# Three seven-product pairs instead of two in each of three FFNs, with some sums made by accumulating transfers

## The chip, the cores and the metric

The kernel runs as one program on one core of a Trainium2 chip. The core has a matrix engine (PE; its weight loads are the row PEld), a vector engine (DVE), a scalar engine (ACT), GpSimd (POOL) and a sync engine (SP), and 16 DMA engines that move data between HBM and the on-chip memory. SP and ACT hand transfers to hardware queues, POOL hands them to a software queue. The metric is device time in microseconds (us) of one execution, as a median over runs.

## The reference

A 256-token, 1024-wide activation goes through three blocks. Each has a mixer and then a gated feed-forward network (FFN); the three FFNs are where the change is made. All arithmetic is float32.

```python
def swiglu(u, w_in, w_out):
    gt, up = jnp.split(u @ w_in, 2, axis=-1)
    return (jax.nn.silu(gt) * up) @ w_out

# layers 0 and 1:  h = h + mixer(rmsnorm(h));  h = h + swiglu(rmsnorm(h, norm_ffn), ffn_w_in, ffn_w_out)
# third block:     x = x + (silu(h2 @ ffn_w1) * (h2 @ ffn_w3)) @ ffn_w2
```

The hidden width is 2816, so an FFN multiplies 256x1024 by 1024x5632 and then 256x2816 by 2816x1024.

## The kernel before, in words

**Units.** Weights come in units of 128 partitions x 1024 floats (512 KB), each as two transfers of 256 KB issued by SP (L466) into a ring of six slots, `raw`. To keep float32 accuracy every unit is split into a high and a low half: ACT writes `whi`, the rounded copy (L631), and DVE then writes `wlo = raw - whi` over `raw` (L1175; the two names share one memory). PE multiplies three times: high by high, activation-low by weight-high, and high by weight-low. So an ordinary unit is 12 matmuls, 8 that need `whi` alone and then 4 that need `wlo` too. Every engine works through the units in one order and counts them in semaphores (`hi_ready`, `lo_ready`, `unit_used`); SP loads unit u once PE has used unit u-6.

**An FFN.** It has 11 blocks of 256 hidden columns. Block j has four "up" units (gate and up columns side by side) and, one block later, two "down" units. `PLAN` writes out the order of all units; ACT, DVE, PE and SP each have a hand-written sequence that follows it (`body`, `pair`, `feed`).

**A pair.** At j in `PAIRED` two neighbouring blocks are done together by a Strassen-type scheme: seven products of half-size operands instead of eight. The four parts of the two blocks' weights (b11, b12, b21, b22, 1 MB each) are loaded into `work` (L510) and DVE makes four sums t1 to t4 from them (L1294, eight instructions of 128x1024 for one pair; t3 takes the place of b12). Each of the seven products is two units of six matmuls (PE lines L2309, L2311, L2314); ACT and DVE split them as they split raw units (L648, L1189). After the 14 half-product units, in whose midst two down units stand, come four up units of block j+2 and four down units. In what follows, b0 to b23 are these 24 units of a pair: b0 to b5, b8 to b15 the half products, b16 to b19 the up units, b20 to b23 the down units. The parts of the second pair are loaded during the first one (`PART_LOADS`).

**Hidden columns.** After each block ACT applies silu, DVE multiplies, PE transposes (`hid_turn`, L2259), ACT copies (L689) and DVE subtracts (L1259); the next down unit waits for that.

**POOL** issues a few loads of tables at the start of the program (L562 to L601) and does nothing in the FFNs.

Of the kernel before, what the change touches and what calls it, by code (L numbers as in the profile page):

```python
# [58 lines left out]
PAIRED = (4, 8)  # L59
# [30 lines left out]

PARTS = [f"{b}_{i}" for b in ("b11", "b12", "b22", "b21") for i in range(2)]
_p0 = plan_at("pair", 0, "b11", 0)
PART_LOADS = {}
for _i, _name in enumerate(PARTS):
    PART_LOADS.setdefault(6 + 2 * _i, []).append((0, _name))
for _i, _name in enumerate(PARTS[:4]):
    PART_LOADS.setdefault(_p0 + 7, []).append((1, _name))
for _i, _name in enumerate(PARTS[4:]):
    PART_LOADS.setdefault(_p0 + 18 + _i, []).append((1, _name))
# [3 lines left out]
for _k in range(len(PAIRED)):  # L103
    SUMS += [f"{_k}_{_t}_{_i}" for _t in ("t1", "t3", "t2", "t4") for _i in range(2)] + [f"{_k}_{_c}" for _c in ("c22", "c11", "c21")]
# [16 lines left out]
              for i, unit in enumerate(PLAN) if unit[0] == "pair"}  # L121

# [128 lines left out]
def build(nc, D, out):  # L251
    with ExitStack() as ctx:
# [28 lines left out]
        rhalf = sb("rhalf", [P, 6, NT])  # L281
        rq_a = sb("rq_a", [P, 64])
# [116 lines left out]

        F_a = W(0, 2048).rearrange("p (k t) -> p k t", k=KT)  # L400
# [18 lines left out]

        def tap(name, n):  # L420
# [8 lines left out]
        half_used = sem("half_used")  # L429
        evac_act, evac_dve = sem("evac_act"), sem("evac_dve")  # L430
# [22 lines left out]
        def _(sp):  # L453
# [33 lines left out]
            def load_ffn(u0, gate_w, gate_n0, up_w, up_n0, down_w):  # L487
# [8 lines left out]
                for i, unit in enumerate(PLAN):  # L496
# [6 lines left out]
                    for pair, name in PART_LOADS.get(i, ()):  # L503
                        b, h = name.split("_")
                        if pair:

                            sp.wait_ge(lo_ready, u0 + plan_at("pair", 0, "t3" if b == "b12" else b, int(h)) + 1)
# [53 lines left out]
        def _(pool):  # L561
# [13 lines left out]
            for half in range(2):  # L575
# [3 lines left out]
            nc.gpsimd.dma_start(A_dec, D["decay"]).then_inc(sem("decay_loaded"), 16)  # L579
            nc.gpsimd.dma_start(posi[:, :], D["positions"][0].rearrange("(t p) -> p t", p=P), allow_slow_non_contiguous=True)\  # L580
                .then_inc(sem("pos_loaded"), 16)
# [16 lines left out]
            for i in range(4):  # L598
# [3 lines left out]
                if i >= 2:  # L602
                    filter_fold(i - 2)


        @block.scalar
        def _(act):
# [25 lines left out]
            def feed(n):  # L633

                for u in range(fed[0], n):
                    if u in PAIR_UNITS:
                        pair_hi(u, *PAIR_UNITS[u])
                    else:
                        split_hi(u % RING, loaded(u), unit_width(u))
                fed[0] = max(fed[0], n)  # L640

            def pair_hi(u, n, k, name, half):
                act.wait_ge(unit_used, u - RING + 1)
                if name[0] == "b":
                    act.wait_ge(part_loaded[name], parts_there(n, k, name))
                else:
                    act.wait_ge(sem("pair_sums"), sums_done(n, f"{k}_{name}_{half}"))
# [32 lines left out]
            def ffn(n, u0, norm):  # L680
# [18 lines left out]
                def silu_of(t, src):  # L699
                    a_(sil[:, t, :], src, ACT.Silu, scale=rstd[:, norm, t:t + 1]).then_inc(sil_ready, 1)  # L700
# [16 lines left out]
                def pair(k, j):  # L717
# [12 lines left out]
                    silu_of(1, F_part[:, 2, 0:256])  # L730
                    feed(b + 17)
                    act.wait_ge(unit_used, b + 14)
                    silu_of(0, ps[0][:, 0:256])
# [4 lines left out]
                    turn(j + 1 + FB * n, 2)  # L738
# [3 lines left out]
                    turn(j + 2 + FB * n)  # L742
                    feed(b + 22)
# [14 lines left out]
                last = u0 + FFN_UNITS - 2  # L758
                feed(last + 2)
                turn(FB * (n + 1), 2)  # L760
                feed(min(last + 5, U_END))
# [399 lines left out]
        def _(dve):  # L1161
# [55 lines left out]
            def row_scale(n):  # L1217
# [3 lines left out]
                rsqrt(rstd[:, n, :], NT)  # L1221
                v_.tensor_scalar(rhalf[:, n, :], rstd[:, n, :], 0.5, None, ALU.mult).then_inc(rstd_ready, 1)
# [27 lines left out]
            def ffn(n, u0, norm, use):  # L1250
# [14 lines left out]
                def token_sum(name):  # L1265
# [6 lines left out]
                    else:  # L1272
                        a11, a12, a21, a22 = (F_a[:, r, c] for c in (slice(0, P), slice(P, S)) for r in (slice(0, 4), slice(4, 8)))
                        x0, x1, op, need = {"s1": (a21, a22, ALU.add, "a1"), "s2": (F_s[:, 0, :, :], a11, ALU.subtract, "s1"),
                                            "s3": (a11, a21, ALU.subtract, "a1"),
                                            "s4": (a12, F_s[:, 1, :, :], ALU.subtract, "s2")}[name]
                        dve.wait_ge(sem("pair_sums"), sums_done(n, need))
                        ins = v_.tensor_tensor(F_s[:, i - 1, :, :], x0, x1, op)
# [7 lines left out]
                def weight_sum(k, name, i):  # L1286

                    x0, x1 = {"t1": ("b12", "b11"), "t3": ("b22", "b12"), "t2": ("b22", "t1"), "t4": ("b21", "t2")}[name]
                    for b in (x0, x1):
                        if b[0] == "b":  # L1290
                            dve.wait_ge(part_loaded[b], parts_there(n, k, b))
                    if x1[0] == "t":
                        dve.wait_ge(sem("pair_sums"), sums_done(n, f"{k}_{x1}_{i}"))
                    v_.tensor_tensor(pair_part(f"{name}_{i}"), pair_part(f"{x0}_{i}"), pair_part(f"{x1}_{i}"), ALU.subtract)\  # L1294
                        .then_inc(sem("pair_sums"), 1)

                def body(j):
                    b = u0 + plan_at("up", j, 0)
                    k = 0 if j < PAIRED[0] else 1
                    away = (PAIRED[k] - j) if j < PAIRED[k] else 0  # L1300
# [11 lines left out]
                    elif away == 2:  # L1312
                        weight_sum(k, "t1", 0)
                        feed(b + 4)
                        weight_sum(k, "t1", 1)
                        feed(b + 5)
                        turn(j + FB * n)
                        feed(b + 6)
                        weight_sum(k, "t3", 0)
                        feed(b + 7)  # L1320
                        hidden(2 * j + 2 * FB * n)
                        weight_sum(k, "t3", 1)
                        return
                    elif away == 1:
                        weight_sum(k, "t2", 0)
                        feed(b + 4)
                        weight_sum(k, "t2", 1)
                        feed(b + 5)
                        turn(j + FB * n)
                        feed(b + 6)  # L1330
                        weight_sum(k, "t4", 0)
                        feed(b + 7)
                        weight_sum(k, "t4", 1)
# [6 lines left out]
                def hid_of(t, src, count):  # L1340
                    dve.wait_ge(sil_ready, count)
                    v_.scalar_tensor_tensor(hid[:, t, :], src, rstd[:, norm, t:t + 1], sil[:, t, :],
# [5 lines left out]
                def pair(k, j):  # L1348
# [13 lines left out]
                    hid_of(1, F_part[:, 2, 256:512], hids + 1)  # L1362
                    feed(b + 16)
                    hid_of(0, ps[0][:, 256:512], hids + 2)
                    feed(b + 17)
                    dve.wait_ge(unit_used, b + 16)
# [8 lines left out]
                    if more:  # L1375
                        weight_sum(k + 1, "t1", 0)
                    feed(b + 20)
                    if more:
                        weight_sum(k + 1, "t1", 1)
                    turn(j + 2 + FB * n)  # L1380
                    feed(b + 21)
                    if more:
                        weight_sum(k + 1, "t3", 0)
# [3 lines left out]
                    if more:  # L1387
                        weight_sum(k + 1, "t3", 1)
# [10 lines left out]
                last = u0 + FFN_UNITS - 2  # L1399
                feed(last + 2)  # L1400
                turn(FB * (n + 1), 2)
                feed(min(last + 5, U_END))
# [17 lines left out]
            v_.memset(sign[0:64, :], 1.0).then_inc(sem("sign_set"), 1)  # L1420
# [1551 lines left out]
```

## Time and profile before

| | |
|---|---|
| median of 3 runs | 1043.28 us (1042.96 to 1043.73) |
| span of the profiled execution | 1041.3 us |
| PE busy | 1033.9 us, 99% of the span, 4884 matmuls and transposes |
| DVE busy | 843.5 us, 81% |
| ACT busy | 593.8 us, 57% |
| POOL busy | 21.6 us, 2% |
| PE clock granted | nine tenths or more in every one of the 40 slices |
| bytes moved | 182.97 MB, 176 GB/s over the span |

The profile is one execution; its page gives the span from the first to the last instruction, 2.0 us under the median of the three runs. PE is busy almost throughout, so time is lost or won where PE does fewer instructions or where it has to wait. Matmuls overlap in the rows: each is shown some 390 ns long while the next begins some 227 ns later, so distances between starts are what counts.

### The profile page before, as it was taken

The numbers are of one execution on the slowest core, as the hardware profiler recorded it, in microseconds if no ns is written. First come the engines' busy times: TensorE is split into PE (matmuls) and PEld (weight loads), VectorE is DVE, ScalarE is ACT, GpSimd is POOL, SyncE is SP. The second block draws the span as 40 slices with busy tenths as digits, with TensorE's granted clock in tenths as the row PEclk, the third lists the DMA queues.
The fourth block names the chain that finished last, engine by engine and source line by source line (L and its number), as shares of the span: only waits on it lengthen the run. The fifth ranks groups of instructions, "written<-read, shape, count | busy, mean of one in ns | idle before, by whom it ended". The sixth has DMA issues, their size and how long they took to land.

```text
span 1041.3 us, 13328 instructions
## 1 busy us (share of the span) xinstructions
PE 1033.9 (99%) x4884; PEld 841.5 (81%) x4884; DVE 843.5 (81%) x1366; ACT 593.8 (57%) x897; POOL 21.6 (2%) x30
## 2 busy tenths in 40 slices
PE   9999999999999999999999999999999999999998
PEld 7877778888888888788888888787777888888887
DVE  6877889797868987896887788989978878878684
ACT  6845474655646646655656564638656446466462
POOL 0221000000000000000000000000000000000000
PEclk9999999999999999999999999999999999999999
DMA  8762478382456534683743653544444468739243
GB/s 278 228 206 83 128 249 270 122 277 87 142 187 187 180 134 142 216 283 126 246 140 96 221 169 122 158 151 154 147 160 135 148 189 258 242 122 303 85 153 107
DMA packets 135706, 182.97 MB, mean 176 GB/s; under 512 B 12588, under 2 KB 82730, under 8 KB 135514
## 3 DMA queue, kind: packets, MB, share of 16 engines
q1 hardware_dynamic: 134130, 178.36, 53.2%
q0 software_dynamic: 1104, 3.21, 1.2%
q8 instruction: 39, 0.64, 0.3%
q10 hardware_dynamic: 408, 0.56, 0.2%
q14 instruction: 25, 0.20, 0.1%
HBM read 181.03 MB, written 1.05 MB: 175 GB/s over the span
## 4 chain that ended last, share of the span: by engine, by line
PE 92%; DVE 5%; ACT 2%; issue 1%; DVEq 0%; ACTq 0%
PE ps L2169 13%; PE ps L2174 13%; PE ps L2170 13%; PE ps L2186 7%; PE ps L2187 7%; PE ps L2191 7%; PE ps L2309 4%; PE ps L2311 4%; PE ps L2314 4%; PE ps L2152 3%; PE ps L2154 3%; PE ps L2153 3%; DVE wlo L1175 1%; PE ps L2259 1%; PE ps L2242 1%; PE ps L2733 1%
## 5 line engine op out<-in xcount | busy, mean ns | idle before, releaser
L1175 DVE TENSOR_TENSOR wlo<-raw,whi 128x1024 fp32r<-128x1024 f32 (+1 forms) x290 | 349.4, 1232 | 28.8 <-ACT whi L631 27.1
L631 ACT ACTIVATE whi<-raw 128x1024 fp32r<-128x1024 f32 (+1 forms) x290 | 295.5, 1053 | 106.9 <-DMA raw<-in_ffn_w_in 33.1
L2169 PE MATMUL ps<-whi,ath 128*128 128x512 f32 (+1 forms) x688 | 274.5, 400 | 2.2 <-ACT whi L631 0.7
L2170 PE MATMUL ps<-whi,atl 128*128 128x512 f32 (+1 forms) x688 | 266.4, 388 | 0.0
L2174 PE MATMUL ps<-wlo,ath 128*128 128x512 f32 (+1 forms) x688 | 182.9, 388 | 0.0
L2169 PEld LDWEIGHTS ps<-whi,ath 128*128 128x128 f32 x688 | 129.3, 188 | 35.6 <-issue 5.9
L2174 PEld LDWEIGHTS ps<-wlo,ath 128*128 128x128 f32 x688 | 128.2, 188 | 27.4 <-DVE wlo L1175 0.6
L2170 PEld LDWEIGHTS ps<-whi,atl 128*128 128x128 f32 x688 | 129.4, 188 | 24.7 <-issue 0.5
L2186 PE MATMUL ps<-whi,brh 128*128 128x512 f32 x272 | 106.5, 392 | 0.0
L2187 PE MATMUL ps<-whi,brl 128*128 128x512 f32 x272 | 105.9, 389 | 0.0
L1189 DVE TENSOR_TENSOR wlo<-work,whi 128x1024 fp32r<-128x1024 f32 x84 | 98.7, 1220 | 4.5 <-ACT whi L648 4.5
L648 ACT ACTIVATE whi<-work 128x1024 fp32r<-128x1024 f32 x84 | 83.8, 1053 | 7.8 <-PE ps L2191 7.8
L2191 PE MATMUL ps<-wlo,brh 128*128 128x512 f32 x272 | 72.7, 389 | 0.0
L1259 DVE TENSOR_TENSOR brl<-ps,brh 128x512 fp32r<-128x512 f32 x33 | 22.7, 689 | 53.3 <-ACT brh L689 53.1
L2186 PEld LDWEIGHTS ps<-whi,brh 128*128 128x128 f32 x272 | 51.1, 188 | 11.1 <-issue 0.3
L2191 PEld LDWEIGHTS ps<-wlo,brh 128*128 128x128 f32 x272 | 51.1, 188 | 10.7
L2187 PEld LDWEIGHTS ps<-whi,brl 128*128 128x128 f32 x272 | 51.1, 188 | 10.3
L1294 DVE TENSOR_TENSOR work<-work 128x1024 f32<-128x1024 f32 x48 | 58.5, 1219 | 0.5 <-DMA work<-in_ffn_w_in 0.4
L689 ACT ACTIVATE brh<-ps 128x512 fp32r<-128x512 f32 x33 | 19.6, 594 | 59.1 <-PE ps L2259 59.1
L655 ACT ACTIVATE ath<-ps,gcol 128x256 fp32r<-128x256 f32 x56 | 22.7, 473 | 37.6 <-PE ps L2242 37.6
L1197 DVE SCALAR_TENSOR_TENSOR atl<-ps,gcol,ath 128x256 fp32r<-128x256 f32 x56 | 23.9, 479 | 21.2 <-ACT ath L655 21.2
L2309 PE MATMUL ps<-whi,sum_hi 128*128 128x512 f32 x96 | 38.0, 396 | 0.0
(380 smaller groups left out, 1415.4 us busy)
## 6 DMA issues: line engine op xcount, KB each, us to landing
raw<-in_ffn_w_in SPq DMA_DIRECT2D x112, 256.0 KB, 3.5
raw<-in_w_in SPq DMA_DIRECT2D x104, 256.0 KB, 2.9
raw<-in_ffn_w SPq DMA_DIRECT2D x100, 256.0 KB, 3.5
raw<-in_ffn_w_out SPq DMA_DIRECT2D x88, 256.0 KB, 3.5
work<-in_ffn_w_in SPq DMA_DIRECT2D x64, 256.0 KB, 4.8
raw<-in_a_w_in SPq DMA_DIRECT2D x48, 256.0 KB, 4.3
raw<-in_b_w_in SPq DMA_DIRECT2D x48, 256.0 KB, 3.1
work<-in_ffn_w SPq DMA_DIRECT2D x32, 256.0 KB, 4.6
```

Of the source, the lines that this page charges most:

```text
L631: a_(unit_view(whi, slot, w), unit_view(raw, slot, w), ACT.Copy).then_inc(hi_ready, 1)
L648: a_(unit_view(whi, u % RING, 512), pair_part(f"{name}_{half}"), ACT.Copy).then_inc(hi_ready, 1)
L1175: v_.tensor_tensor(unit_view(wlo, slot, w), unit_view(raw, slot, w), unit_view(whi, slot, w), ALU.subtract).then_inc(lo_ready, 1)
L1189: v_.tensor_tensor(unit_view(wlo, u % RING, 512), pair_part(f"{name}_{half}"), unit_view(whi, u % RING, 512), ALU.subtract).then_inc(lo_re ...
L1294: v_.tensor_tensor(pair_part(f"{name}_{i}"), pair_part(f"{x0}_{i}"), pair_part(f"{x1}_{i}"), ALU.subtract)\
L2169: mm(ps[bk + apart * t][:, 0:w], ath[:, k, t * P:(t + 1) * P], rh[:, kk, :], start=k == 0, stop=False)
L2170: mm(ps[bk + apart * t][:, 0:w], atl[:, k, t * P:(t + 1) * P], rh[:, kk, :], start=False, stop=False)
L2174: ins = mm(ps[bk + apart * t][:, 0:w], ath[:, k, t * P:(t + 1) * P], rl[:, kk, :], start=False, stop=k == KT - 1)
L2186: mm(o, act_h[:, k, t * P:(t + 1) * P], rh[:, nb, :], start=first, stop=False)
L2187: mm(o, act_l[:, k, t * P:(t + 1) * P], rh[:, nb, :], start=False, stop=False)
L2191: ins = mm(ps[banks[2 * nb + t]][:, :], act_h[:, k, t * P:(t + 1) * P], rl[:, nb, :], start=False, stop=last)
L2309: mm(ps[bank][:, :], hi[:, 2 * i + kk, :], rh[:, kk, :], start=not onto and i + kk == 0, stop=False, skip_group_check=onto)
```

## The change

It changes the three FFNs, and four things in them.

1. `PAIRED` goes from (4, 8) to (3, 6, 9): three pairs in each FFN. After a pair the next one follows at once, and the last pair has no up units behind it, so its two blocks' down units come straight after its products.
2. The signs of the sums are turned so that t1, t2 and t4 are plain additions of whole parts: three DVE instructions of 128x2048 for one pair instead of eight of 128x1024. Two of the products come out negated, and `rneg`, the negated row scale, puts that right.
3. t3 = b12 + b22 is made by POOL: one accumulating transfer of 1 MB from on-chip memory to on-chip memory.
4. For the two down units b20 and b21 after the first and the second pair of each FFN (`ADDED`, 12 units in all) DVE's subtraction is left out. ACT writes `wlo = -whi` over `raw`, and POOL then adds the weights again from HBM onto it, by two accumulating transfers of 256 KB for each unit. PE waits for these transfers in `low_there`.

The parts of the next pair are also asked for at other places of SP's order, and some semaphores of the mixers are merged.

```diff
-PAIRED = (4, 8)
+PAIRED = (3, 6, 9)
+
+ACC_ROW = 2048
...
-            plan += [("up", j + 2, c) for c in range(4)]
-            plan += [("down", j + b, k) for b in range(2) for k in range(2)]
+            if j + 2 < FB:
+                plan += [("up", j + 2, c) for c in range(4)]
+                plan += [("down", j + b, k) for b in range(2) for k in range(2)]
+            else:
+                plan += [("down", j, k) for k in range(2)]
...
+for _k in range(len(PAIRED)):
+    _at = (6, 7, 8, 9, 10, 11, 13, 15)
+    if _k:
+        _at = [plan_at("pair", _k - 1, "b11", 0) + n for n in (8, 9, 10, 11, 17, 18, 19, 20)]
+    for _i, _name in zip(_at, PARTS):
+        PART_LOADS.setdefault(_i, []).append((_k, _name))
...
+ADDED = [u0 + plan_at("pair", k, "b11", 0) + i for u0 in (U_F0, U_F1, U_F2) for k, j in enumerate(PAIRED) if j + 2 < FB
+         for i in (20, 21)]
...
+            def add_low(n, k):
...
+                for m, u in enumerate(ADDED):
+                    if first <= u < first + 24:
+                        pool.wait_ge(neg_ready, m + 1)
+                        if m >= 2:
+                            pool.wait_ge(lo_added[m % 2], 32 * (m // 2))
+                        _, j, k2 = PLAN[u - (U_F0, U_F1, U_F2)[n]]
+                        v, row = unit_view(wlo, u % RING, 512), (2 * j + k2) * P
+                        for nb in range(2):
+                            nc.gpsimd.dma_start(v[:, nb, :], down_w[row:row + P, nb * 512:(nb + 1) * 512],
+                                                accum_op=ALU.add).then_inc(lo_added[m % 2], 16)
+
+            for n in range(3):
+                for k in range(len(PAIRED)):
+                    pool.wait_ge(sem("pair_sums"), sums_done(n, f"{k}_t1"))
+                    pool.wait_ge(part_loaded["b22"], parts_there(n, k, "b22"))
+                    nc.gpsimd.dma_start(pair_whole("t3"), pair_whole("b22"), accum_op=ALU.add, max_dma_last_dim=ACC_ROW)\
+                        .then_inc(sem("pair_t3_added"), 16)
+                    add_low(n, k)
...
+                    if u in ADDED:
+                        a_(unit_view(wlo, u % RING, 512), unit_view(raw, u % RING, 512), ACT.Copy, scale=-1.0)\
+                            .then_inc(neg_ready, 1)
...
+                elif name == "t3":
+                    act.wait_ge(sem("pair_t3_added"), t3_there(n, k))
...
-                    else:
+                    elif u not in ADDED:
                         split_lo(u % RING, u + 1, unit_width(u))
...
+            def low_there(n):
+
+                if n - 1 in ADDED:
+                    m = ADDED.index(n - 1)
+                    pe.wait_ge(lo_added[m % 2], 32 * (m // 2 + 1))
+                else:
+                    pe.wait_ge(lo_ready, low(n))
...
+                    if j + 2 == FB:
+                        product(b + 14, 1, *a22, onto=True, middle=lambda: hid_turn(hids + 2))
+                        pe.wait_ge(hid_lo, j + 1 + FB * n)
+                        down_unit((b + 16) % RING, 2, False, False, b + 17, brh, brl)
+                        hid_turn(hids + 4)
+                        down_unit((b + 17) % RING, 3, False, False, b + 18, brh, brl)
+                        return
```

How the order moves is seen at three places. The first is SP's queue around the end of the first pair of the first FFN, before: `raw<-` are a unit's two transfers, `work<-` the two of half a part of the next pair.

```order
L466 DMA raw<-in_ffn_w_in 128x2x256 x6
L510 DMA work<-in_ffn_w_in 128x2x256 x2
L466 DMA raw<-in_ffn_w_in 128x2x256 x2
L510 DMA work<-in_ffn_w_in 128x2x256 x2
L466 DMA raw<-in_ffn_w_out 128x512 x2
L510 DMA work<-in_ffn_w_in 128x2x256 x2
L466 DMA raw<-in_ffn_w_out 128x512 x2
```

And the same place now.

```order
L488 DMA raw<-in_ffn_w_in 128x2x256 x4
L534 DMA work<-in_ffn_w_in 128x2x256 x2
L488 DMA raw<-in_ffn_w_in 128x2x256 x2
L534 DMA work<-in_ffn_w_in 128x2x256 x2
L488 DMA raw<-in_ffn_w_in 128x2x256 x2
L534 DMA work<-in_ffn_w_in 128x2x256 x2
L488 DMA raw<-in_ffn_w_out 128x512 x2
L534 DMA work<-in_ffn_w_in 128x2x256 x2
L488 DMA raw<-in_ffn_w_out 128x512 x10
```

Before b20, the first `in_ffn_w_out` unit, SP asked for six others of 512 KB from b16 on (four up units, two halves of parts); now for seven (four and three). Before b21 it was eight, and is nine.

The second place is ACT at the same point, before, from the last two up units of the pair on (`brh` is the turned hidden block, `sil` the silu).

```order
L631 ACTIVATE whi<-raw 128x1024 x2
L689 ACTIVATE brh<-ps 128x512
L631 ACTIVATE whi<-raw 128x1024 x2
L700 ACTIVATE sil<-ps,rstd 128x256 x2
L631 ACTIVATE whi<-raw 128x1024 x7
```

And now.

```order
L679 ACTIVATE whi<-raw 128x1024 x2
L742 ACTIVATE brh<-ps 128x512
L679 ACTIVATE whi<-raw 128x1024
L689 ACTIVATE wlo<-raw 128x1024
L679 ACTIVATE whi<-raw 128x1024
L689 ACTIVATE wlo<-raw 128x1024
L753 ACTIVATE sil<-ps,rstd 128x256 x2
L679 ACTIVATE whi<-raw 128x1024 x2
L701 ACTIVATE whi<-work 128x1024 x6
```

Behind each high half of b20 and b21 stands its negated copy, and the next pair's parts (`whi<-work`) follow after b22 and b23.

The third place is POOL's queue in the FFNs, of which nothing stood there before; these are the rows of the first FFN and the first row of the next.

```order
+L649 DMA work<-work 128x4x512
+L642 DMA wlo<-in_ffn_w_out 128x512 x4
+L649 DMA work<-work 128x4x512
+L642 DMA wlo<-in_ffn_w_out 128x512 x4
+L649 DMA work<-work 128x4x512 x2
```

The t3 of the second and of the third pair (`work<-work`) are issued behind the four additions of the pair ahead of each; POOL takes them in this order alone.

## Rows read from the trace of the kernel before

**Rows 1.** The page: busy time, clock, and the chain that ended last.

```profile
PE 1033.9 (99%) x4884; PEld 841.5 (81%) x4884; DVE 843.5 (81%) x1366; ACT 593.8 (57%) x897; POOL 21.6 (2%) x30
...
PEclk9999999999999999999999999999999999999999
...
PE 92%; DVE 5%; ACT 2%; issue 1%; DVEq 0%; ACTq 0%
```

**Rows 2.** Timeline of PE, low products of b20 and b21 (start, length).

```profile
232.27 1.07 PE L2191 MATMUL ps<-wlo,brh 128*128 128x512 f32 x4
...
234.99 0.39 PE L2191 MATMUL ps<-wlo,brh 128*128 128x512 f32 x1
```

**Rows 3.** Timeline of ACT: high halves of b20 and b21 in the first pair.

```profile
225.17 0.60 ACT L689 ACTIVATE brh<-ps 128x512 fp32r<-128x512 f32 x1 [0.94 <-PE ps L2259]
226.01 1.06 ACT L631 ACTIVATE whi<-raw 128x1024 fp32r<-128x1024 f32 x1 [0.24 <-DMA raw<-in_ffn_w_out]
228.87 1.06 ACT L631 ACTIVATE whi<-raw 128x1024 fp32r<-128x1024 f32 x1 [1.79 <-DMA raw<-in_ffn_w_out]
```

**Rows 4.** Timeline of SP's queue: b16 to b18 asked for, later b20.

```profile
212.01 3.60 SPq L466 DMA_DIRECT2D raw<-in_ffn_w_in  x6
...
218.73 1.45 SPq L466 DMA_DIRECT2D raw<-in_ffn_w_out  x2
```

**Rows 5.** Windows: busy time in each, PE clock, share of the DMA engines, GB/s.

```profile
193.30:241.30 48.00, 48.00 (x219) 39.73 (x218) 39.17 (x42) 29.05 (x35) 0.00 (x0) 1.00 0.76 250
220.00:232.00 12.00, 12.00 (x56) 9.94 (x55) 11.64 (x14) 6.73 (x10) 0.00 (x0) 1.00 1.07 370
26.00:40.00 14.00, 14.00 (x92) 11.94 (x91) 10.73 (x22) 9.09 (x13) 7.80 (x15) 1.00 1.01 280
52.00:60.00 8.00, 8.00 (x35) 5.77 (x34) 6.53 (x8) 3.53 (x5) 1.07 (x2) 1.00 0.78 226
```

**Rows 6.** Timeline of ACT: two high halves in a row.

```profile
211.15 2.00 ACT L648 ACTIVATE whi<-work 128x1024 fp32r<-128x1024 f32 x2
```

**Rows 7.** POOL's transfers: size, median us from issue to landing.

```profile
con<-in_consts POOLq DMA_DIRECT2D x4, 290.0 KB, 3.2
...
work<-in_decay POOLq DMA_DIRECT2D x1, 512.0 KB, 7.9
```

**Rows 8.** Line L576, POOL's two loads of 512 KB: issue (ns, starts), landing.

```profile
L576 POOL DMA_DIRECT2D work<-in_filt_w x2: 523/524/526, 25.6 to 26.1; - x2
...
DMA to landing us min/median/max: 5.2/6.2/7.2
```

**Rows 9.** Timelines of POOL and DVE while POOL issues a transfer.

```profile
53.20 0.54 POOL L601 DMA_DIRECT2D con<-in_consts  x1 [17.86 <-DVE work L1485]
...
52.82 2.35 DVE L1175 TENSOR_TENSOR wlo<-raw,whi 128x1024 fp32r<-128x1024 f32 x2
```

**Rows 10.** Groups of DVE's instructions in the whole run (count, busy, mean ns).

```profile
L1175 DVE TENSOR_TENSOR wlo<-raw,whi 128x1024 fp32r<-128x1024 f32 (+1 forms) x290 | 349.4, 1232 | 28.8 <-ACT whi L631 27.1
L1189 DVE TENSOR_TENSOR wlo<-work,whi 128x1024 fp32r<-128x1024 f32 x84 | 98.7, 1220 | 4.5 <-ACT whi L648 4.5
L1294 DVE TENSOR_TENSOR work<-work 128x1024 f32<-128x1024 f32 x48 | 58.5, 1219 | 0.5 <-DMA work<-in_ffn_w_in 0.4
```

**Rows 11.** Timelines of PE and DVE at the end of the second pair's products.

```profile
281.75 0.39 PE L2309 MATMUL ps<-whi,ath 128*128 128x512 f32 x1
...
281.39 0.48 DVE L1342 SCALAR_TENSOR_TENSOR hid<-ps,rstd,sil 128x256 f32<-128x256 f32 x1 [1.31 <-ACT sil L700]
```

**Rows 12.** Timeline of PE and DVE: first matmul after b23; a sum for the next pair.

```profile
241.34 0.39 PE L2169 MATMUL ps<-whi,ath 128*128 128x512 f32 x1
...
223.29 1.22 DVE L1294 TENSOR_TENSOR work<-work 128x1024 f32<-128x1024 f32 x1
```

More of the change, by code:

```diff
@@ L91 @@
 PARTS = [f"{b}_{i}" for b in ("b11", "b12", "b22", "b21") for i in range(2)]
-_p0 = plan_at("pair", 0, "b11", 0)
 PART_LOADS = {}
[L94 to L99, printed above, removed]
+for _k in range(len(PAIRED)):
[4 more added lines that the diff above has]
+        PART_LOADS.setdefault(_i, []).append((_k, _name))
 SUMS = ["a0", "a1", "s1", "s2", "s3", "s4", "l1", "l2", "l3", "l4"]
 for _k in range(len(PAIRED)):
-    SUMS += [f"{_k}_{_t}_{_i}" for _t in ("t1", "t3", "t2", "t4") for _i in range(2)] + [f"{_k}_{_c}" for _c in ("c22", "c11", "c21")]
+    SUMS += [f"{_k}_{_t}" for _t in ("t1", "t2", "t4")] + [f"{_k}_{_c}" for _c in ("c22", "c11", "c21")]
 COPIES = 4 + 3 * len(PAIRED)
@@ L121, with low @@
               for i, unit in enumerate(PLAN) if unit[0] == "pair"}
+ADDED = [u0 + plan_at("pair", k, "b11", 0) + i for u0 in (U_F0, U_F1, U_F2) for k, j in enumerate(PAIRED) if j + 2 < FB
+         for i in (20, 21)]
+assert all(PLAN[(u - U_F0) % (U_F1 - U_F0)][0] == "down" for u in ADDED if u < U_B)
+def low(n):
+    return n - sum(u < n for u in ADDED)
 C_COLS = ((768, 512), (1280, 512), (0, 512), (512, 256), (1792, 512), (2304, 512), (2816, 512), (3328, 512))
@@ L281, in build @@
         rhalf = sb("rhalf", [P, 6, NT])
+        rneg = sb("rneg", [P, 6, NT])
         rq_a = sb("rq_a", [P, 64])
@@ L429, in build @@
         half_used = sem("half_used")
+        neg_ready, lo_added = sem("neg_ready"), [sem(f"lo_added{i}") for i in range(2)]
         evac_act, evac_dve = sem("evac_act"), sem("evac_dve")
@@ L505, in load_ffn @@
                         if pair:
-                            sp.wait_ge(lo_ready, u0 + plan_at("pair", 0, "t3" if b == "b12" else b, int(h)) + 1)
+                            sp.wait_ge(lo_ready, low(u0 + plan_at("pair", pair - 1, "t3" if b == "b12" else b, int(h)) + 1))
+                            if b == "b21":
+                                sp.wait_ge(sem("pair_sums"), sums_done(n, f"{pair - 1}_t4"))
                         block = PAIRED[pair] + (b[2] == "1")
@@ L603, in _ @@
                     filter_fold(i - 2)
+            def add_low(n, k):
+                down_w = (D["ffn_w_out"][0], D["ffn_w_out"][1], D["ffn_w2_2"][0])[n]
+                first = (U_F0, U_F1, U_F2)[n] + plan_at("pair", k, "b11", 0)
+                for m, u in enumerate(ADDED):
[15 more added lines that the diff above has]
+                    add_low(n, k)
         @block.scalar
@@ L757, in ffn @@
                         j += 1
[L758 to L761, printed above, removed]
+                feed(min(u0 + FFN_UNITS + 3, U_END))
             def stage(use, scale, n, u0, ahead=4):
@@ L1398, in ffn @@
                         j += 1
[L1399 to L1402, printed above, removed]
+                feed(min(u0 + FFN_UNITS + 3, U_END))
             def turns(arg, k, cos, red):
@@ L2170, in up_unit @@
                     mm(ps[bk + apart * t][:, 0:w], atl[:, k, t * P:(t + 1) * P], rh[:, kk, :], start=False, stop=False)
-                pe.wait_ge(lo_ready, ready)
+                low_there(ready)
                 for kk, t in parts:
@@ L2187, in down_unit @@
                         mm(o, act_l[:, k, t * P:(t + 1) * P], rh[:, nb, :], start=False, stop=False)
-                pe.wait_ge(lo_ready, ready)
+                low_there(ready)
                 for nb in range(2):
@@ L2301, in body, with product @@
                             ffn_down(j, c - 4, j + FB * n, u % RING, u + 1, j == 1 and c == 4, False)
-                def product(u, bank, hi, lo, onto=False):
+                def product(u, bank, hi, lo, onto=False, middle=None):
                     for i in range(2):
+                        if i and middle is not None:
+                            middle()
                         pe.wait_ge(hi_ready, u + i + 1)
@@ L2368, in ffn @@
                 pe.wait_ge(hid_lo, FB * (n + 1))
-                end = [(last, 2, False, False), (last + 1, 3, False, True)]
+                end = [(last, 0, False, False), (last + 1, 1, False, True)]
                 if r < 4:
```

141 lines of the change are left out of this document (69 added, 72 removed).

## The prediction

> **What bounds the kernel now.** I read the page first: PE is busy 99% of the span at full clock, and the chain that ended last is 92% PE [rows 1]. So the time is the number of PE's instructions times their spacing, plus whatever PE has to wait; DVE (81%) and ACT (57%) matter only where they are late. Then I read the 48 us from the start of the first pair of the first FFN to its last down unit: PE busy 48.00 of 48.00, DVE 39.17, ACT 29.05 [rows 5] (its first line). No wait of PE is left there that a lighter DVE could give back. Then I asked how late each thing that PE needs arrives at b20 and b21, because there the change swaps a DVE instruction for a chain through ACT, POOL and the DMA engines. Last come the DMA engines: in the 12 us in which b20 and b21 land they are fully taken, share 1.07 at 370 GB/s [rows 5] (its second line).
>
> **What goes.** A pair turns 96 matmuls into 14 units of six, 84. There is one pair more in each of three FFNs, so 36 matmuls go. The low products of two neighbouring down units begin at 232.27 and 234.99, 2.72 us apart for 12 matmuls, 0.227 us each [rows 2]. 36 x 0.227 = 8.2 us, all of it on PE's path, as PE does not wait there. This is all the change can win on that path.
>
> **DVE and ACT.** One more pair means six more units to split in each FFN, 1.2 us of DVE and 1.05 us of ACT each, and the 16 sums of 1.22 us per FFN become nine of twice the length, 2.3 to 2.4 us [rows 10]. Against that, four subtractions in each FFN go. From pair to pair, now 48 us of PE apart, DVE has 22 subtractions (25 to 27 us), three long sums (7), and some 7 us of partial sums, hidden products and turned blocks: 39 to 41 us, what it also has in the stretch that I read (39.17 of 48). ACT has its 29.05 and two more copies of 1.05. Neither becomes the bound, and I cost both at nothing: PE's 48 us hide them. If that cover were gone, each us over 48 would cost six times a us.
>
> **The low halves of b20 and b21.** This decides. Before, the data of b20 land at 226.0 (ACT starts then, having waited for the DMA), those of b21 at 228.87, again after a wait for the DMA [rows 3], and PE wants their low halves at 232.27 and 234.99 [rows 2]. DVE had more than 3 us to spare. Step by step, in the times of this trace:
> - SP asks for one more 512 KB ahead of b20 and of b21 than before (the order in SP's queue). From b20 to b21 two such pieces landed in 2.86 us, 1.43 us each [rows 3], the queue being backed up: b20 was asked for at 218.73 [rows 4] and took 7.3 us. So b20 lands at 227.44, b21 at 230.30.
> - ACT makes the high half and then the negated copy. Two such passes take 2.00 us [rows 6]: 229.44 and 232.3.
> - POOL issues two transfers of 256 KB. What these take, no row shows: the trace holds no accumulating transfer. Bounds by the nearest rows: four loads of 290 KB on POOL's queue landed 3.2 us after issue [rows 7], beside a DMA share of 0.78 [rows 5] (its last line); POOL's two loads of 512 KB landed after 5.2 and 7.2 us [rows 8] and a third after 7.9 [rows 7], beside a share of 1.01 [rows 5] (its third line). With the second issue 0.54 us behind the first [rows 9], the small load gives 229.44 + 0.54 + 3.2 = 233.2, 0.9 us after PE wants it; the large ones 234.6 and 237.3, 2.4 and 5.1 us late. Below, 0: if the data came sooner than I count, PE would not wait at all, and it cannot gain more, as it waits for nothing here now.
> - I take 5.2 us, so 2.4 us late: it is the row with the right size (512 KB), on the same queue, beside full DMA engines, with nothing of POOL's ahead of it.
> - b21 then: 232.3 + 5.2 = 237.5, wanted at 234.99 + 2.4 = 237.4. Its wait is inside the first.
>
> While PE waits at b20, b21 to b23 and all later units queue behind it; nothing catches that up, since PE has no idle time later. Six pairs have such units (two in each FFN): 6 x 2.4 = 14.2 us; bounds 0, 5.4 and 30.4.
>
> The Trainium skill has a rule against this (Collectives: The Full Stack, "The bandwidth ceiling: the fold count and why AG ≠ RS ≠ AR"): a transfer that adds needs two reads for each write and so moves at half the rate of a copy. No run here shows it yet; by it 5.2 becomes up to 10.4 us, 7.6 us late, and the sum an estimated 1082.
>
> A second rule (SBUF — State Buffer, "SBUF: two separate sides") says that POOL can't write the descriptors of its transfers while DVE runs a mode that takes the port the two share. The trace does not bear it out for the subtractions that fill DVE here: POOL issued at 53.20 inside two of them, in 0.54 us, and they took 2.35 us, no longer than elsewhere [rows 9], so I add nothing.
>
> **The sum t3.** POOL issues t3 of the next pair behind the additions of b21, at 232.3 + 1.1 = 233.4. t1, for which it waits too, is there earlier: its first half began at 223.29 [rows 12], and the whole ends some 2.4 us later. The next pair begins where now a plain block follows, at 241.34 [rows 12] + 2.4 = 243.7; ACT needs t3 1.0 us ahead of the third half product, 2.7 us in: by 245.4. Two 512 KB loads, 1 MB, took from 25.6 to 26.1 + 7.2 = 33.3, so 7.7 us [rows 8]; behind b21's landing that is 245.2. It is hidden, with 0.2 us to spare by the slow rows and more by the fast ones, SP's queue being nearly empty then. If it were twice as slow, 7.5 us at each of six places. The first pair's t3 has the time of some seven units.
>
> **The end of an FFN.** The last pair has no up units to hide its last two blocks. The block to be transposed between the halves of the last product is ready at 281.39 + 0.48 = 281.87, and PE would begin at 281.75 and load weights ahead of that [rows 11]: about 0.5 us, with the next waits inside it. Three FFNs: 1.5 us, between 0 and 3.
>
> **The sum.** The span is 1041.3 us, 2.0 under the median, which I keep as it is. 1043.3 - 8.2 + 14.2 + 1.5 = 1050.8.
>
> **The rivals.**
> - The transfers are in time: POOL's land sooner, or b20's data do, and nothing waits for them. For it: the 36 matmuls certainly go, and an order with 0.9 us missing by the fast rows needs little help. Against it: three waits in a row (DMA, ACT, POOL) where DVE alone had 3 us. The time: 1043.3 - 8.2 + 0 to 3, 1035 to 1038, or up to 1041 with half a us at each place. Chance 0.22.
> - The isolated row holds: 0.9 us late. 1043.3 - 8.2 + 5.4 + 1.5 = 1042.0, no change that can be told. Against it: the DMA engines aren't as free as they were beside that row. Chance 0.15.
> - Adding costs up to twice a copy. The place is PE's wait at b20, and past 12 us for 1 MB also at t3; it decides from about 8 us for 512 KB on. The time: 1067 by the 7.9 us row (1043.3 - 8.2 + 30.4 + 1.5), 1082 by twice the 5.2 us row (7.6 us late six times, 45.6 us), more if t3 is late as well. The first rule above speaks for it. The add must also read what it adds to. Against: the DMA engines have room after SP's burst. Chance 0.16.
> - My forecast, 1.4 to 5.1 us late at each of six places, 1045 to 1067: 0.47.
>
> **How the numbers follow.** 0.2% is 2.1 us, about what a measurement of this kernel can tell. Faster (under 1041.2): the first rival and a sliver of the second, 0.25. The same (to 1045.4): most of the second, 0.12. Slower: 0.63. The likeliest case gives 1050.8, its own range 1045 to 1067. The range of 8 in 10 takes in the transfers in time at the low end and the slow row at the high end, 1036 to 1072, and leaves out about 0.05 below and 0.13 above.
>
> **What would show it.** 36 matmuls fewer on PE. A wait of PE ahead of the low products of b20, ended by POOL's transfer into `wlo`, six times, 2.4 us each; nearly none ahead of b21's. The landing of those transfers, 5.2 us; of t3, under 12 us, and no wait of ACT for it that reaches PE. b20's data landing 1.4 us later in its pair than before. If PE shows no wait at b20, the step of the landing is wrong and the time is under 1041; if the longest wait is at t3 or at DVE, my place is wrong.

## The result

The changed kernel takes 1074.67 us, the median of 4 runs (1073.98 to 1078.9), beside 1043.43 for the kernel before in the same session: ratio 1.031, 95% interval 1.0298 to 1.0322. It is slower, by 31.2 us; 7.5 slower was forecast, and the range ended at 1072.

The page of the changed kernel answers to [rows 1]; its profiled execution took 1073.98 us, with a span of 1072.1:

```profile
PE 1039.3 (97%) x4848; PEld 839.9 (78%) x4848; DVE 858.7 (80%) x1366; ACT 625.8 (58%) x936; POOL 54.6 (5%) x63
...
PEclk9999999989899999999999999999999999999999
...
PE 76%; DMA 8%; DVE 8%; ACT 3%; SPq 3%; issue 1%; POOL 0%; DVEq 0%; ACTq 0%
```

The 36 matmuls are gone (4884 to 4848), and yet PE is busy longer. The chain holds transfers and SP's queue, which it did not before, and two slices show a lower clock. What PE waited for (us in total, times, longest):

```profile
PE ps L2242 <- DMA wlo<-in_ffn_w_out: 14.7, 5, 3.8
PE ps L2242 <- DMA wlo<-in_ffn_w: 8.4, 3, 4.3
PE ps L2293 <- DVE x L1293: 2.2, 2, 1.1
```

L2242 are the low products of a down unit. So 23.1 us of waits stand where they were expected, ahead of the low halves that POOL's transfers make: six at b20 and two at b21. The first pair, on PE, ACT and POOL (answers to [rows 2, 3, 9]):

```profile
215.23 0.39 PE L2238 MATMUL ps<-whi,brl 128*128 128x512 f32 x1
219.15 2.07 PE L2242 MATMUL ps<-wlo,brh 128*128 128x512 f32 x4 [3.53 <-DMA wlo<-in_ffn_w_out]
221.02 0.63 PE L2237 MATMUL ps<-whi,brh 128*128 128x512 f32 x1
221.45 0.63 PE L2238 MATMUL ps<-whi,brl 128*128 128x512 f32 x1
...
224.44 1.52 PE L2242 MATMUL ps<-wlo,brh 128*128 128x512 f32 x4
```

```profile
210.39 1.06 ACT L679 ACTIVATE whi<-raw 128x1024 fp32r<-128x1024 f32 x1 [1.34 <-DMA raw<-in_ffn_w_out]
211.35 1.04 ACT L689 ACTIVATE wlo<-raw 128x1024 fp32r<-128x1024 f32 x1
214.15 1.06 ACT L679 ACTIVATE whi<-raw 128x1024 fp32r<-128x1024 f32 x1 [1.75 <-DMA raw<-in_ffn_w_out]
```

```profile
212.70 1.77 POOL L642 DMA_DIRECT2D wlo<-in_ffn_w_out  x2 [46.69 <-ACT wlo L689]
```

Read it from top to bottom in time: ACT has the raw tile at 210.39, after a wait for it, the negated copy is done at 212.39, POOL writes its two transfers until 214.47, PE has done its high products by 215.6 and starts the low ones at 219.15. The four low products then take 2.07 us, those of b21 1.52, where [rows 2] has 1.07. Windows of the changed kernel show why (the first number is the window's length; behind POOL stand the granted clock, the DMA engines' busy share and GB/s):

```profile
215.20:219.20 4.00, 0.47 (x3) 0.05 (x1) 2.65 (x3) 4.00 (x7) 2.75 (x3) 0.91 0.97 174
218.50:225.40 6.90, 6.25 (x15) 4.90 (x16) 5.67 (x5) 2.16 (x3) 1.00 (x1) 0.51 1.09 189
...
273.10:279.90 6.80, 6.09 (x14) 4.80 (x15) 5.51 (x5) 2.00 (x3) 0.86 (x1) 0.50 1.00 175
522.30:525.70 3.40, 3.40 (x8) 2.74 (x9) 3.40 (x4) 0.64 (x1) 0.00 (x0) 0.50 1.10 190
1020.65:1024.06 3.41, 3.13 (x7) 2.51 (x8) 3.41 (x4) 1.41 (x2) 0.27 (x1) 0.50 1.05 177
```

PE had stood still since about 215.6 when, at 218.5, the clock fell from 2.4 to 1.2 GHz. Four of the six places have such a stretch, 20.5 us in all. Matmuls follow each other there by 0.43 us (221.02 to 221.45) instead of 0.227. Half of the 20.5 us would be 10.2, but PE stands waiting in a part of them; counted by the 43 weight loads at the wider spacing, 8.4 us are lost.

POOL's transfers, size and median us to landing (answer to [rows 7]):

```profile
work<-work POOLq DMA_DIRECT2D x9, 1024.0 KB, 10.4
wlo<-in_ffn_w_out POOLq DMA_DIRECT2D x16, 256.0 KB, 5.2
wlo<-in_ffn_w POOLq DMA_DIRECT2D x8, 256.0 KB, 5.1
con<-in_consts POOLq DMA_DIRECT2D x4, 290.0 KB, 3.3
```

And of the line that issues the 24 additions, the issue in ns (min, median, max; the sixteen of FFN 0 and 1), then us to landing:

```profile
L642 POOL DMA_DIRECT2D wlo<-in_ffn_w_out x16: 852/930/1232, 212.7 to 572.9; - x16
...
DMA to landing us min/median/max: 4.0/5.2/6.1
```

An adding transfer of 256 KB takes 5.2 us in the median where a copy of 290 KB takes 3.3. At the end of FFN 0, the timeline of DVE shows the wait that stands in the third line of PE's waits:

```profile
317.38 4.62 DVE L1230 TENSOR_TENSOR wlo<-raw,whi 128x1024 fp32r<-128x1024 f32 x4
321.92 1.28 DVE L1293 TENSOR_TENSOR x<-x,ps 128x512 f32<-128x512 f32 x2
```

DVE makes four low halves, three of them of the next stage, before it adds the residual whose block PE transposes next.

The account, with waits measured from weight load to weight load less their spacing of 0.23 us (so that the refilling behind a wait is in it): 1043.4 - 8.2 (matmuls) + 24.2 (six waits at b20) + 1.9 (two at b21) + 8.4 (clock) + 2.2 (the residual at two FFN ends, gaps of 1.73 and 1.71 where the kernel before has 0.63 each) + 2.1 (the last pair's products in three FFNs and the down unit behind them, six gaps of 0.40 to 0.68) + 0.7 (one wait behind t3) = 1074.7, measured 1074.7. The profiled execution, from which the terms are read, took 1074.0, so some 0.7 us are counted too much.

### The profile page after: what moved, and what is told of

It is laid out like the page before. It is cut to its first block, busy times and chain, and to the rows that moved or that the text cites. A ratio compares the mean times of both kernels' runs of the same rounds, so it can differ in the third digit from the quotient of the medians.

```text
span 1072.1 us, 13395 instructions
## 1 busy us (share of the span) xinstructions
PE 1039.3 (97%) x4848; PEld 839.9 (78%) x4848; DVE 858.7 (80%) x1366; ACT 625.8 (58%) x936; POOL 54.6 (5%) x63
## 4 chain that ended last, share of the span: by engine, by line
PE 76%; DMA 8%; DVE 8%; ACT 3%; SPq 3%; issue 1%; POOL 0%; DVEq 0%; ACTq 0%
PE ps L2220 9%; PE ps L2225 9%; PE ps L2221 8%; PE ps L2242 7%; PE ps L2237 6%; PE ps L2238 6%; PE ps L2365 4%; PE ps L2360 4%; PE ps L2362 4%; DMA raw<-in_ffn_w_out 3%; DVE wlo L1230 3%; PE ps L2195 2%; PE ps L2197 2%; PE ps L2196 2%; DMA wlo<-in_ffn_w_out 2%; SPq L488 2%
## 5 line engine op out<-in xcount | busy, mean ns | idle before, releaser
L679 ACT ACTIVATE whi<-raw 128x1024 fp32r<-128x1024 f32 (+2 forms) x266 | 271.6, 1052 | 121.8 <-DMA raw<-in_ffn_w_in 34.6
L1230 DVE TENSOR_TENSOR wlo<-raw,whi 128x1024 fp32r<-128x1024 f32 (+2 forms) x254 | 305.8, 1233 | 26.4 <-ACT whi L679 25.6
L2220 PE MATMUL ps<-whi,ath 128*128 128x512 f32 (+1 forms) x592 | 236.5, 400 | 1.8 <-DVE atl L1252 0.8
L2221 PE MATMUL ps<-whi,atl 128*128 128x512 f32 (+1 forms) x592 | 229.0, 388 | 0.0
L1244 DVE TENSOR_TENSOR wlo<-work,whi 128x1024 fp32r<-128x1024 f32 x126 | 147.8, 1220 | 35.4 <-ACT whi L701 35.4
L701 ACT ACTIVATE whi<-work 128x1024 fp32r<-128x1024 f32 x126 | 125.6, 1051 | 54.9 <-DMA work<-work 47.2
L2225 PE MATMUL ps<-wlo,ath 128*128 128x512 f32 (+1 forms) x592 | 157.2, 387 | 0.0
L2242 PE MATMUL ps<-wlo,brh 128*128 128x512 f32 x272 | 78.1, 411 | 23.0 <-DMA wlo<-in_ffn_w_out 14.7
L2242 PEld LDWEIGHTS ps<-wlo,brh 128*128 128x128 f32 x272 | 53.3, 199 | 37.5 <-DMA wlo<-in_ffn_w_out 16.8
L1353 DVE TENSOR_TENSOR work<-work 128x2048 f32<-128x2048 f32 x27 | 61.6, 2283 | 0.0
L2362 PE MATMUL ps<-whi,sum_lo 128*128 128x512 f32 x144 | 56.1, 390 | 0.0
L2365 PE MATMUL ps<-wlo,sum_hi 128*128 128x512 f32 x144 | 44.5, 391 | 0.3 <-DVE wlo L1244 0.3
```

Of the source, the lines that this page charges most:

```text
L679: a_(unit_view(whi, slot, w), unit_view(raw, slot, w), ACT.Copy).then_inc(hi_ready, 1)
L701: a_(unit_view(whi, u % RING, 512), pair_part(f"{name}_{half}"), ACT.Copy).then_inc(hi_ready, 1)
L1230: v_.tensor_tensor(unit_view(wlo, slot, w), unit_view(raw, slot, w), unit_view(whi, slot, w), ALU.subtract).then_inc(lo_ready, 1)
L1244: v_.tensor_tensor(unit_view(wlo, u % RING, 512), pair_part(f"{name}_{half}"), unit_view(whi, u % RING, 512), ALU.subtract).then_inc(lo_re ...
L2220: mm(ps[bk + apart * t][:, 0:w], ath[:, k, t * P:(t + 1) * P], rh[:, kk, :], start=k == 0, stop=False)
L2221: mm(ps[bk + apart * t][:, 0:w], atl[:, k, t * P:(t + 1) * P], rh[:, kk, :], start=False, stop=False)
```

## The experiments

The theory: everything lost comes from the six places where PE waits for the chain raw tile, ACT, POOL, transfer, and from the clock that falls there. Rivals: three pairs are too much for DVE (1), the 1 MB sums or the traffic slow it (2), it is the adding itself and not the length of the chain (3). Times of before in these sessions were 1043.0 to 1043.2.

**All low halves back on DVE.**

```
-ADDED = [u0 + plan_at("pair", k, "b11", 0) + i for u0 in (U_F0, U_F1, U_F2) ... for i in (20, 21)]
+ADDED = []
```

> All 12 low halves back on DVE, three pairs and the accumulating 1 MB sums kept. Theory (the waits of PE at the low products of b20 and the fall of the granted clock behind them are the whole loss): 1074.7 - 26 (waits) - 10.2 (clock) = 1038.5, between 1036 and 1042, with no record at clock 0.5 inside the FFNs; what is left over 1035 is the 3.0 us at the two FFN ends. Rival 1 (DVE can't carry three pairs without being relieved): PE waits for DVE's wlo instead, 1050 or more. Rival 2 (the 1 MB sums or the added DMA traffic are what slows the kernel): 1060 or more.

Measured: 1040.58 us (1039.64 to 1041.91, 10 runs), ratio 0.9976 (0.9967 to 0.9986) to before. No stretch at the lower clock, no wait of a down unit's low half over 0.5 us. As the theory says, and 34.1 us under the changed kernel. Rival 1 falls as long as the 1 MB sums are made by transfers, and rival 2 as far as these sums go; the traffic of the low halves' transfers went with them here, so this run alone does not clear it.

**t3 by DVE, the accumulating low halves kept.**

```
-nc.gpsimd.dma_start(pair_whole("t3"), pair_whole("b22"), accum_op=ALU.add, max_dma_last_dim=ACC_ROW)...
...
+v_.tensor_tensor(pair_whole("t3"), pair_whole("t3"), pair_whole("b22"), ALU.add)...
```

The second line stands in DVE's order, behind t1.

> The sum of t3 by DVE (one more addition over 2048 columns per pair, nine in all), the accumulating low halves kept. Theory: the waits at b20 stay and the time is 1070 to 1077. Rival 2 (the 1 MB accumulating transfers are the cause, by their own waits or by crowding the queue): below 1055. Rival 1 (DVE is full): over 1080.

Measured: 1078.32 us (1076.44 to 1080.69). The waits for the low halves are still there (23.2 us in six). The clock fell at all six places instead of four. 1.3 us over the range that I gave the theory, but far from rival 2.

**Both by DVE.** The two edits above together.

> Three pairs per FFN and nothing by accumulating transfers: DVE makes all low halves and all sums. Theory: DVE has room, because with the low halves alone given back PE waited for it nowhere inside an FFN; within 2 us of that run's 1040.6, so 1039 to 1043. Rival 1 (DVE can't carry three pairs): the nine sums of 2.2 us more make its low halves late, over 1045.

Measured: 1047.25 us (1046.93 to 1047.87), ratio 1.0039 (1.0024 to 1.0054). My expectation failed here. PE's waits name the reason:

```profile
PE ps L2249 <- DVE wlo L1227: 5.7, 6, 1.1
```

```profile
222.14 1.19 PE L2249 MATMUL ps<-wlo,brh 128*128 128x512 f32 x4 [0.92 <-DVE wlo L1227]
```

Six waits, now for DVE itself, and not at b20 and b21, whose low products start on time in the first pair (215.62 and 218.34), but at b22 (second fence): DVE makes its low half at 220.87, behind the long sums. The 1 MB transfers are thus worth 6.7 us (1047.25 to 1040.58): three pairs without any help for DVE are slower than two. DVE, which I had costed at nothing, has room for the 12 low halves or for the nine sums, not for both.

**The 24 transfers copy instead of adding.**

```
-    nc.gpsimd.dma_start(v[:, nb, :], down_w[...], accum_op=ALU.add)...
+    nc.gpsimd.dma_start(v[:, nb, :], down_w[...])...
```

> The 24 transfers of the 12 low halves copy the weights instead of adding them (so these low halves hold the whole weight), same place in the chain, same size. Theory (what is late is the chain: landing of the raw tile, two ACT copies, two issues of POOL, a transfer of about 5 us whatever it does): landing 4.5 to 5.2 us each, 1068 to 1075. Rival 3 (the adding, with its second read, makes the landing long): landing near the 3.2 us of the 290 KB constants, 2 us less at each of six places and a shorter fall of the clock, 1050 to 1062.

Measured: 1059.27 us (1056.93 to 1061.31), in rival 3's range and under the theory's. POOL's transfers and its two issues at the first b20:

```profile
wlo<-in_ffn_w_out POOLq DMA_DIRECT2D x16, 256.0 KB, 3.3
wlo<-in_ffn_w POOLq DMA_DIRECT2D x8, 256.0 KB, 3.2
```

```profile
213.73 1.10 POOL L642 DMA_DIRECT2D wlo<-in_ffn_w_out  x2 [48.21 <-ACT wlo L689]
```

The transfer is 1.9 us shorter and the two issues 0.7 us (1.77 to 1.10). So rival 3 holds for 15.4 of the 31 us, in which stands a shorter fall of the clock (three stretches of 3.4 us, where adding has 20.5 in four). 14.4 us of waits in six are there for a copy too: they belong to the chain as a whole, of which the copy is the last link. From the end of ACT's negated copy to PE's start it takes 4.9 us in the mean of the six places, with adding 6.3.

**PE kept busy in the wait.** 16 matmuls into a free bank between the high and the low products of b20.

```
+    for _ in range(idle):                      # 16 at b20, none elsewhere
+        mm(ps[1][:, :], act_h[:, k, 0:P], rh[:, 0, :], start=True, stop=True)
     low_there(ready)
```

> The changed kernel, with 16 matmuls more at each of the 12 places, between the high and the low products of b20, into a free PSUM bank that is written anew before it is read; 16 x 0.227 = 3.6 us of work inside a wait of about 4.1 us. Theory (the fall of the clock follows from PE's standing still in that wait): no stretch at clock 0.5 behind b20, the waits' end where it was, 1074.7 - 10.2 = 1064.5, between 1062 and 1068. Rival (the clock falls for another reason, load or transfers): stretches at 0.5 remain, 1073 to 1080.

Measured: 1068.31 us (1067.58 to 1069.72), 0.3 over the range. (The matmuls stand at six places, 96 in all; the 12 of the expectation are the units of `ADDED`.) The clock stays at full speed in all slices, and PE waits for:

```profile
PEclk9999999999999999999999999999999999999999
```

```profile
PE ps L2244 <- DMA wlo<-in_ffn_w_out: 3.1, 7, 0.7
...
PE ps L2244 <- DMA wlo<-in_ffn_w: 1.7, 2, 1.3
```

The added matmuls (96 x 0.227 = 21.8 us) and the waits left (4.8) are 3.5 us more than the 23.1 us of waits they stand for, as at full speed PE comes earlier to b21 and waits there; the kernel is 6.4 us faster all the same. So the clock took 9.9 us by itself by the medians; by the two profiled executions (1073.98 and 1069.72), from which the waits are read, 7.8, against 8.4 counted by weight loads. And in this kernel it does not fall where PE works through the wait.

**Three high blocks first.**

```
-for c in range(4):
+for c, part in ((0, "hi"), (1, "hi"), (2, "hi"), (0, "lo"), (1, "lo"), (2, "lo"), (3, None)):
...
```

`down_unit` does the high products, the low ones, or, with None and in the changed kernel, both.

> Only PE's order changes: the high products of b20, b21 and b22 come first, then the low products of b20, b21, b22, then b23. Two more blocks of eight matmuls, 3.6 us, lie between the point where PE waited and the first low product. Theory: of the 4.1 us per place about 0.5 is left, the clock stays at 1.0, and the time is 1037 to 1044. If a raw tile or a slot of the ring comes late by the later release of b20, a part of the wait comes back at another place, up to 1050. Rival 2 (sums and traffic): no change, 1065 or more.

Measured: 1065.06 us (1063.0 to 1066.24). A miss. PE's timeline in the first pair:

```profile
220.92 1.07 PE L2245 MATMUL ps<-wlo,brh 128*128 128x512 f32 x4
223.80 2.53 PE L2245 MATMUL ps<-wlo,brh 128*128 128x512 f32 x8 [1.81 <-DMA wlo<-in_ffn_w_out]
```

b20's low half is now in time. But b21's is made one chain later, and PE, which needed 2.7 us from one to the other, now asks for it 0.9 us behind: the wait moved to b21 (12.7 us in six), and the clock fell behind it at four places.

**All four high blocks first**, and the same with the residual moved (last experiment).

```
-for c in range(4):
+for c, part in ((0, "hi"), (1, "hi"), (2, "hi"), (3, "hi"), (0, "lo"), (1, "lo"), (2, "lo"), (3, "lo")):
...
```

> Accumulating transfers as in the changed kernel; PE makes the high products of all four down units b20 to b23 first, then the four low ones. With three high blocks ahead (the earlier run) the first low block was in time and the wait had moved to b21, whose low half landed 21.9 us after the pair's first turned block, where PE asked for it at about 20. One more high block puts that to 21.8. Theory: the waits for the transfers fall from 2.4 to under 0.5 us at each place, no stretch at clock 0.5, 1038.5 + 6 x 0.7 (PE waits for ACT's high halves of b22) = 1042.7, between 1040 and 1046. Rival (the ring's later release delays the next pair): 1050 or more.

> The same with the residual ahead of the next stage's low halves at the end of FFN 0 and 1, an edit that gave 0.6 us where DVE made all low halves: 0.5 to 2 us under the run with four high blocks first. If DVE's relief by the transfers is worth anything once PE doesn't wait for them, this run is under the 1040.0 of the kernel with all low halves by DVE and the same edit; the theory says it isn't: 1040 to 1045.

Measured: 1062.51 us (1059.49 to 1066.4) and 1060.13 (1058.93 to 1061.25). The waits for the low halves are all but gone and the clock is at full speed, as expected, but both times lie far over the ranges of the theory, the first in that of the rival. In the run with four high blocks PE and ACT wait for:

```profile
PE ps L2368 <- DVE wlo L1244: 6.9, 6, 1.2
...
PE ps L2245 <- DMA wlo<-in_ffn_w_out: 1.7, 2, 1.5
```

```profile
ACT whi L701 <- DMA work<-work: 44.8, 6, 8.2
```

```profile
227.96 3.90 ACT L701 ACTIVATE whi<-work 128x1024 fp32r<-128x1024 f32 x4 [7.12 <-DMA work<-work]
```

L2368 is a half product of the next pair, L1244 its low half, L701 its high half, and `work<-work` is t3. In the first pair ACT has t3 at 227.96, and PE starts the product that needs it at 229.16: PE now comes to t3 as t3 lands. t3 was hidden, as predicted, but behind the very wait that this order removes. By weight loads PE loses 17.5 us more here than with DVE's low halves; the largest group, six gaps of 1.77 us at L2368, makes 9.3 of them, and the others are not traced. No run parts t3 from the later release of the ring's slots, which the rival named, so the cause is open here.

**The parts behind b21 and b22**, so that the raw tiles of b20 and b21 land sooner; then the same with a quarter of these parts' bytes.

```
-_at = [... + n for n in (8, 9, 10, 11, 17, 18, 19, 20)]
+_at = [... + n for n in (8, 9, 10, 11, 21, 21, 22, 22)]
```

```
+if pair and b in ("b21", "b22"):
+    dst, src = dst[:, 0:1, 0:128], src[:, 0:1, 0:128]
```

The second edit is in the second run only; b21 and b22 are parts of the weights there.

> SP issues the last four parts of the next pair's weights behind the raw tiles of b21 and b22 instead of ahead of b20 and b21. Theory (the raw tile of b20 is late behind these parts in SP's queue): the raw tile lands up to 4.3 us earlier, but ACT reaches it only 1.3 us earlier, as it has a turn ahead; 1.3 us less at each of the four to six places that have parts there, and a shorter fall of the clock, 1060 to 1069. Rival 2 (the transfers only change places): the parts come late for DVE's sums t1 and t2 and PE waits for these, 1073 or more.

> The parts issued behind b21 and b22, as in the earlier run, and these four parts of the second and third pair at a quarter of their bytes (the rest of those weights stays as it was). In the earlier run ACT's chain was 1.9 us earlier and the additions landed 6.9 us after issue instead of 5.2, so that PE's wait ended where it had. Theory (the additions and the parts share the DMA engines): landing back at 5.2 or less, PE's wait 1.7 to 2 us shorter at each of six places and fewer stretches at clock 0.5, 1055 to 1064. Rival (an addition takes its time whatever runs beside it, and the wait ends late for another reason): landing 6.9, 1070 or more.

Measured: 1073.47 us (1070.76 to 1077.51), nothing gained, and 1055.38 (1053.9 to 1059.6), in the range. The first is the number of its rival 2, but not its cause: PE waits for no sum, the waits for the low halves stay (22.3 us in six), and the clock fell at all six places. In the first, POOL issues and PE goes on at:

```profile
211.06 3.61 POOL L642 DMA_DIRECT2D wlo<-in_ffn_w_out  x4 [45.16 <-ACT wlo L689]
```

```profile
219.45 2.07 PE L2242 MATMUL ps<-wlo,brh 128*128 128x512 f32 x4 [3.92 <-DMA wlo<-in_ffn_w_out]
```

```profile
wlo<-in_ffn_w_out POOLq DMA_DIRECT2D x16, 256.0 KB, 6.9
```

The additions start 1.6 us earlier than in the changed kernel (211.06, not 212.70) and land no sooner, 6.9 us after issue. With the parts cut to a quarter:

```profile
wlo<-in_ffn_w_out POOLq DMA_DIRECT2D x16, 256.0 KB, 5.9
wlo<-in_ffn_w POOLq DMA_DIRECT2D x8, 256.0 KB, 5.6
```

The waits shrink to 11.9 us in ten, none of them with a fall of the clock behind it. So both things are true of the chain: the raw tile is late behind the parts in SP's queue, and an adding transfer that runs beside those parts pays for it instead. The landing did not come all the way back to 5.2, which I had expected: 1.0 of the 1.7 us did.

**DVE's low halves, the residual first.** From the first experiment; at the end of FFN 0 and 1 DVE adds the residual before the next stage's second and third low half.

```
-feed(u0 + first)
+feed(u0 + (1 if u0 in (U_B, U_C) else first))
 residual(0, half_used, halves, banks)
+feed(u0 + first)
...
-feed(min(u0 + FFN_UNITS + 3, U_END))
+feed(min(u0 + FFN_UNITS + 1, U_END))
```

> All low halves by DVE, 1 MB sums by transfer, and at the end of FFN 0 and 1 DVE makes the residual of the first half ahead of the low halves of the next stage's second and third unit. Theory: the two waits of x_turn (1.73 us between weight loads, 1.5 beyond their spacing) go, 1040.6 - 3.0 = 1037.6, between 1036.5 and 1039. Rival: these low halves are then late for PE, and 1040 or more.

Measured: 1039.97 us (1039.37 to 1041.09, 7 runs), ratio 0.997 (0.9959 to 0.9982): the fastest kernel here, but 0.6 us under the first experiment, not 3.0, and the two ranges overlap. The waits of x_turn, PE's transposes of the new residual (L2293 above), are gone: the two gaps ahead of it shrink from 1.73 to 0.63 us, which the kernel before has too, so 2.2 us and not 3.0 were there to gain. In their place the next units wait longer for turned blocks, which DVE now makes behind two low halves; the two gaps ahead of these units grow from 0.8 to 1.4 us:

```profile
PE ps L2220 <- DVE atl L1251: 2.3, 3, 0.8
```

## Why the prediction was right and wrong

- **The place and the mechanism** were right: PE waits ahead of the low products of b20, six times, for POOL's transfer into `wlo`. So was the gain (36 matmuls, 8.2 us), and so, nearly, were the first steps of the chain: the high half starts 4.8 us ahead of PE's need by the forecast and 5.1 in the first pair, and the negated copy is done 2.0 us later in both. The 5.1 is luck: the six places have 4.3 in the mean (by weight loads), and in five other runs with the same order up to there ACT has the first tile 0.8 to 2.0 us later. This makes 0.5 us at each place, some 3 in all.
- **One step that failed is the landing.** I let both transfers land 5.2 us after the negated copy, by a row of a 512 KB copy. In the first pair it is 219.15 - 212.39 = 6.8 us: 0.3 to start POOL, some 0.6 until its second issue begins, and 5.9 from there. The six places have 6.3 in the mean, 1.1 more than forecast, 6.7 us in all. The size was right and the kind wrong: with copies the same way takes 4.9 us in the mean, near the forecast, and one transfer 3.3 to landing, where adding has 6.3 and 5.2. POOL's longer issue (0.9 against 0.55) hardly counts, as the second issue begins 0.6 us behind the first in both. Together with the tile's 3 us this made 24.2 out of 14.2. My third rival, adding dearer than a copy (1067 to 1082, given 0.16), was the case; but its number was met only with the clock's help, which it does not have in it: 1074.7 - 8.4 = 1066.3. The Trainium skill's rule that an add has two reads and moves at half the rate (Collectives: The Full Stack, "The bandwidth ceiling: the fold count and why AG ≠ RS ≠ AR"), stated there for the reducing step of a ring, points the right way; the landing here grew by 5.2 / 3.3 = 1.6, not by 2.
- **b21's wait inside b20's**: right in four pairs of six; 1.9 us more in the other two.
- **The other step that failed: a wait of PE was priced by its length alone**, and the clock behind it at nothing, without a reason: 8.4 us. The kernel before never lets PE stand still like this inside an FFN, so no row of it shows the fall. The first wait, 3.5 us, cost 2.8 more behind it. Without these 8.4 us, or without the landings' 6.7, the time would have been in the range that I gave.
- **t3 hidden under 12 us**: right, 10.4 us (7.7 by the row of copies) and one wait of 0.7. Behind the additions it is so only as PE is late itself: with four high blocks first PE comes to t3 as it lands.
- **DVE at nothing**: right for this change, with little to spare: with low halves and sums both on DVE, six waits and 6.7 us.
- **The end of an FFN**: 1.5 us forecast at the last pair's products, 2.1 measured there. Another 2.2 stand at a place that I did not name, the residual of FFN 0 and 1.
- **The sum**: the 23.9 us between 1050.8 and 1074.7 are 11.9 (waits for the low halves: 6.7 by the landings, some 3 by the tiles, 1.9 at b21), 8.4 (clock), 2.8 (FFN ends) and 0.7 (t3).

## What to carry to other kernels

Work that an engine does in time costs nothing; handed to a chain of three engines and a queue it must be timed from end to end, and each transfer priced by a row of its own kind, adding or copying. In a kernel that PE bounds, price a wait by its length and by a half-speed stretch that may follow it (here at four of six). Before an order is changed to hide one wait, look for what that wait hides.

## What the runs showed of the hardware

- An adding transfer from DRAM into SBUF, 256 KB: 5.2 us to landing in the median (4.0 to 6.1) and 0.85 to 1.23 us of POOL for the issue; the same as a copy, 3.3 and 0.53 to 0.58. With the parts issued beside it 6.9. A 1 MB addition within SBUF: 10.4 us, and 2.0 us of issue.
- While the additions run, the DMA engines are as busy as before and move half, each added byte counted once: in the changed kernel 371 GB/s at a share of 1.09 from 205 to 212 us, 174 at 0.97 from 215.2 to 219.2 (in the copying run, beside the copies, 197 at 0.62 from 214.5 to 217.5):

```profile
205.00:212.00 7.00, 7.00 (x34) 5.81 (x33) 6.76 (x6) 3.58 (x5) 0.00 (x0) 1.00 1.09 371
```

- The granted clock fell to 1.2 GHz at four of the six waits, whose idle time was 3.5 us in the first, and stayed there for 3.4 or 6.8 us. With three high blocks first it fell behind an idle time of 1.8 us too (223.80 in its timeline above), with two of 0.6 us ahead of it.
